# Two transformer blocks on one core: earlier weight loads, both roots ahead of the mixers' tiles, two blocks tile by tile, gate rows in one block

## The reference

```python
def first_block(x, c, ...):                    # 512 tokens, D = 1024
    sh1, sc1, g1, sh2, sc2, g2 = split(silu(c) @ w_ada + b_ada, 6)
    h = rmsnorm(x, norm_attn_g) * (1 + sc1) + sh1
    proj = h @ w_in                            # 3*512 + 4*512 columns, and 8 + 8 for beta and alpha
    y = concat([dilated_attention(...), gated_deltanet(..., beta, alpha)]) @ w_out
    x = x + g1 * y
    h = rmsnorm(x, norm_ffn_g) * (1 + sc2) + sh2
    x = x + g2 * ((silu(h @ w_gate) * (h @ w_up)) @ w_down)
    return rmsnorm(x, final_norm_g)

def second_block(x, c, ctx, c_ctx, ...):       # 512 tokens (main) and 256 (ctx)
    for i in range(2):
        m, mc = the 9 modulations of c and of c_ctx: silu(.) @ w_ada[i] + b_ada[i]
        h, hc = h + 0.5*m[2]*swiglu(norm(h)*(1+m[1])+m[0]), the same for hc     # ffn1, hidden 2816
        z  = (norm(h)*(1+m[4])+m[3]) @ w_in[i]
        zc = the same for hc; in the last layer only the columns of keys and values
        y = concat([fourier, latent attention, spatial gating, pooling])(z, zc) @ w_out[i]
        h = h + m[5]*y;  h = h + 0.5*m[8]*swiglu(norm(h)*(1+m[7])+m[6])         # ffn2
        # hc likewise, except in the last layer
    return rms_norm(h, g_final)
```

## Time and profile before

| | |
|---|---|
| time, median of 3 runs | 3936.7 us (3933.88 to 3936.72) |
| the profiled execution's own time | 3945.08 us |
| its span | 3943.0 us |
| TensorE busy | 3641.0 us, 92% |
| VectorE busy | 2209.7 us, 56% |
| ScalarE busy | 1039.1 us, 26% |
| mean granted TensorE clock | 0.950 of full |
| DMA | 335.83 MB, mean 85 GB/s |

### The profile page before, as it was taken

The page is one execution under the profiler, slowest core; times in us unless marked ns, Lnnn a source line. Parts: engine busy times, 40 slices in busy tenths (PEclk is TensorE's granted clock), DMA queues, the critical chain, the costliest instruction groups (busy, mean ns, idle before and its releaser), DMA issues. The chain is left out here.

```text
span 3943.0 us, 47361 instructions
## 1 busy us (share of the span) xinstructions
PE 3641.0 (92%) x19168; PEld 2981.5 (76%) x19168; DVE 2209.7 (56%) x5139; ACT 1039.1 (26%) x1620; POOL 184.4 (5%) x155
## 2 busy tenths in 40 slices
PE   5898998899989999969999999998999996889998
PEld 3755886788778888856477888887888885568886
DVE  5555555755655656655436666676666535544334
ACT  2354002322332121223333112123212124333222
POOL 1012101000010000010010000010000010000000
PEclk9999887999989999979899999998999998999999
DMA  5533002444323424322012333433343312113332
GB/s 164 153 90 85 1 1 65 118 120 121 107 70 94 113 83 118 90 83 66 11 38 70 92 110 93 113 91 90 87 113 91 107 43 67 57 48 90 95 90 67
DMA packets 636620, 335.83 MB, mean 85 GB/s; under 512 B 20564, under 2 KB 631864, under 8 KB 636145
## 3 DMA queue, kind: packets, MB, share of 16 engines
q1 hardware_dynamic: 635248, 330.19, 29.6%
q10 hardware_dynamic: 1152, 2.62, 0.2%
HBM read 328.05 MB, written 4.72 MB: 84 GB/s over the span
## 5 line engine op out<-in xcount | busy, mean ns | idle before, releaser
L1874 PE MATMUL psum<-hn_high,high 128*128 128x512 f32 (+3 forms) x3336 | 1207.1, 362 | 16.9 <-DVE hn_low L2286 10.4
L1876 PE MATMUL psum<-hn_high,low 128*128 128x512 f32 (+3 forms) x3336 | 1188.2, 356 | 0.0
L1875 PE MATMUL psum<-hn_low,high 128*128 128x512 f32 (+3 forms) x3336 | 1186.2, 356 | 0.0
L1874 PEld LDWEIGHTS psum<-hn_high,high 128*128 128x128 f32 (+2 forms) x3336 | 632.7, 190 | 128.3 <-DVE hn_low L2286 19.2
L1876 PEld LDWEIGHTS psum<-hn_high,low 128*128 128x128 f32 (+2 forms) x3336 | 630.8, 189 | 97.4 <-issue 0.9
L1875 PEld LDWEIGHTS psum<-hn_low,high 128*128 128x128 f32 (+2 forms) x3336 | 631.5, 189 | 90.1 <-issue 0.5
L2311 DVE SCALAR_TENSOR_TENSOR partial<-stage,cond,partial 128x128 f32<-128x128 f32 x2304 | 625.4, 348 | 0.0
L2255 DVE TENSOR_TENSOR low<-stage,high 128x1024 fp32r<-128x1024 f32 (+2 forms) x416 | 498.3, 1218 | 198.5 <-ACT high L1580 198.0
L1580 ACT ACTIVATE high<-stage 128x1024 fp32r<-128x1024 f32 (+2 forms) x416 | 415.5, 1022 | 548.2 <-DMA stage<-in_w_ffn 365.6
L1874 PE MATMUL psum<-hidden_high,high 128*128 128x512 f32 (+1 forms) x1408 | 502.6, 357 | 4.0 <-DVE low L2255 4.0
L1876 PE MATMUL psum<-hidden_high,low 128*128 128x512 f32 (+1 forms) x1408 | 496.1, 352 | 0.0
(11 more groups left out here) (293 smaller groups left out, 3111.4 us busy)
## 6 DMA issues: line engine op xcount, KB each, us to landing
stage<-in_w_ffn SPq DMA_DIRECT2D x240, 512.0 KB, 4.4
stage<-in_w_ada SPq DMA_DIRECT2D x192, 512.0 KB, 4.0
stage<-in_w_in SPq DMA_DIRECT2D x48, 512.0 KB, 5.2
stage<-in_w_out SPq DMA_DIRECT2D x24, 512.0 KB, 4.3
stage<-in_w_ffn SPq DMA_DIRECT2D x32, 384.0 KB, 3.8
stage<-in_w_gate SPq DMA_DIRECT2D x22, 512.0 KB, 4.0
stage<-in_w_up SPq DMA_DIRECT2D x22, 512.0 KB, 5.2
stage<-in_w_down SPq DMA_DIRECT2D x16, 512.0 KB, 4.2
```

The source lines that it names most:

```text
L1874: self.e.matmul(out, high[:, i], xh, start=first and n == 0, stop=False)
L1875: self.e.matmul(out, high[:, i], xl, start=False, stop=False)
L1876: done = self.e.matmul(out, low[:, i], xh, start=False, stop=last and n == nk - 1)
```

## The change

1. **Loads apart from splits.** `load()` issues a block's DMA alone; `load_to(target)` issues loads up to a target as long as a stage is free; `weights()` brings one split block ahead as before, and lets the DMA of one more go.
2. **Norm.** `modulated_norm` brings one block ahead of the root and the second behind it. In `mixers` both roots are taken first, one block is brought ahead of them, `load_mixer`, tables and `clear_pool` come after them, and then the tiles of both parts.
3. **Last square.** The eighth square is no longer added by POOL: PE's `sum_squares` sums `mean_main` (seven squares) and then the last square itself into the same PSUM columns.
4. **Tile by tile in turn.** `products_by_tile` makes the products of two blocks in one pass over the feature tiles: three matmuls of one bank, three of the other. It is used for the gates with qk 0, for gate and up of each swiglu's first group, and for the first two blocks of the mixers.
5. **Gates.** One block of 40 columns: beta in rows 0 to 7, alpha in rows 32 to 39 (and beta's columns once more between them as filling). `gate_rows` now follows qk 0's products. With one call less, the modulations' pumps shift by three.

```diff
-    def bring(self, n):
+    def load(self, n):
...
         self.load_block(n, stage, moves)
+        return stage, raw
+
+    def load_to(self, target):
+
+        while self.loaded <= target and not self.stages.peek().taken:
+            self.landing[self.loaded] = self.load(self.loaded)
+            self.loaded += 1
...
-        self.bring_to(target)
+        later = self.split_after(n + 1)
+        self.bring_to(later[0] if split and later else n)
+        if len(later) > 1:
+            self.load_to(later[1])
...
-            t.free = [("squares", name, k)]
-        part.squares = ("squares", name, k)
-        part.unfinished = k == KT - 1
+            if k < KT - 1:
+                t.free = [("squares", name, k)]
+            else:
+                part.unfinished = t
...
-        self.bring_two()
-        rinv, ready, t = self.residual_root(part, name)
+        self.bring_next(1)
+        rinv, ready, t = root or self.residual_root(part, name)
+        self.bring_next(2)
...
-        for n, name in enumerate(("beta", "alpha")):
...
-            self.linear(name, w, KT, 3584 + 8 * n, 8, part, take_gate)
+        gates, qk = ((3584, 16), (3584, 16), (3592, 8)), ((0, P),)
...
+        self.products_by_tile(keys, [two[0].ap[0:40], two[1].ap], [x[0] for x in asked], [x[2] for x in asked], main.hn,
+                              main.hn_ready)
...
+        for name, row in (("beta", 0), ("alpha", 32)):
+            self.gate_row(name, two[0].ap[row:row + 8], keys[0])
...
-                    self.products(("gate_sum", key), bank_a.ap[:, 0:T], n_a, wa, part.hn, 0, [],
-                                  each=part.hn_ready if at == 0 else None)
...
+                    if at == 0:
+                        self.open_sum(bank_b)
+                        self.products_by_tile([("gate_sum", key), ("up_sum", key)], [bank_a.ap[:, 0:T], bank_b.ap[:, 0:T]],
+                                              [n_a, n_b], [wa, wb], part.hn, part.hn_ready)
...
-        self.load_mixer(layer, base)
+        self.bring_next(1)
+        roots = {}
         for part in both:
...
-            if part in full:
-                self.load_tables(m)
-                self.clear_pool(m)
...
-            self.modulated_norm(name, part, mem.gain[:, :, part.col:part.col + 1], rows(part, 3), [("gain", name)])
+            roots[part.name] = self.residual_root(part, name)
+        self.load_mixer(layer, base)
+        for part in full:
+            m = mem.mixer[part.name]
+            self.load_tables(m)
+            self.clear_pool(m)
+        for part in both:
+            name = ("mix", layer, part.name)
+            self.modulated_norm(name, part, mem.gain[:, :, part.col:part.col + 1], rows(part, 3), [("gain", name)],
+                                root=roots[part.name])
...
+    def products_by_tile(self, keys, outs, numbers, views, x, each):
+
+        nk = len(each)
+        for i in range(nk):
+            for key, out, n, (high, low) in zip(keys, outs, numbers, views):
+                self.wait_ge("split", n)
+                self.wait_ge(*each[i])
+                xh, xl = x[0][:, i, 0:out.shape[1]], x[1][:, i, 0:out.shape[1]]
+                self.e.matmul(out, high[:, i], xh, start=i == 0, stop=False)
+                self.e.matmul(out, high[:, i], xl, start=False, stop=False)
+                done = self.e.matmul(out, low[:, i], xh, start=False, stop=i == nk - 1)
...
-    def sum_squares(self, name, part, bank):
-
-        self.wait_ge(*part.squares)
+    def sum_squares(self, name, part, bank, last):
+
+        self.wait_ge("squares", name, KT - 2)
         self.wait_free(bank)
         for a in range(part.T // P):
-            done = self.e.matmul(bank.ap[:, a:a + 1], part.mean[:, a * P:(a + 1) * P], self.mem.ones[:, 0:1], start=True, stop=True)
+            self.e.matmul(bank.ap[:, a:a + 1], part.mean[:, a * P:(a + 1) * P], self.mem.ones[:, 0:1], start=a == 0, stop=False,
+                          skip_group_check=True)
+        self.wait_ge("square", name, KT - 1)
+        for a in range(part.T // P):
+            done = self.e.matmul(bank.ap[:, a:a + 1], last[:, a * P:(a + 1) * P], self.mem.ones[:, 0:1], start=False, stop=True,
+                                 skip_group_check=True)
```

More of the change, by code:

```diff
@@ L513, in bring_to, with bring_next @@
             self.brought += 1
[L515 to L519, removed]
+    def bring_next(self, count):
+        if self.board.plan is not None:
+            later = self.split_after(len(self.asked))
+            if later:
+                self.bring_to(later[min(count, len(later)) - 1])
+            if len(later) > 1:
+                self.load_to(later[1])
     def pieces(self, name, sources):
@@ L1080, in sections, with opened @@
         w = self.mem.inp["w_in_2"][layer]
-        def product(block, part, n, view, first):
+        def opened(block, part):
             kind, f, columns, _, put = block
             cols = sum(width for _, width in columns)
-            bank, key = self.banks.next(), (kind, layer, part.name, f)
+            bank, key = self.banks.next(), ("sum", (kind, layer, part.name, f))
             self.open_sum(bank)
             out = bank.ap[0:cols, 0:part.T]
-            self.products(("sum", key), out, n, view, part.hn, 0, [] if first else part.hn_ready,
-                          each=part.hn_ready if first else None)
-            return lambda: put(part, f, out, ("sum", key), bank)
-        done = []
-        asked = [self.weights(w, 0, KT, columns, sum(width for _, width in columns)) for _, _, columns, _, _ in blocks[:2]]
-        parts = blocks[0][3]
-        for part in parts:
-            for n, block in enumerate(blocks[:2]):
-                number, slot, view = asked[n]
-                done.append(product(block, part, number, view, n == 0))
-                if part is parts[-1]:
-                    slot.free = [("sum", (block[0], layer, part.name, block[1]))]
-            for take in done:
+            return key, out, lambda: put(part, f, out, key, bank)
+        two = blocks[:2]
+        asked = [self.weights(w, 0, KT, columns, sum(width for _, width in columns)) for _, _, columns, _, _ in two]
+        for part in two[0][3]:
+            keys, outs, takes = zip(*[opened(block, part) for block in two])
+            self.products_by_tile(keys, outs, [x[0] for x in asked], [x[2] for x in asked], part.hn, part.hn_ready)
+            for key, (_, slot, _) in zip(keys, asked):
+                if part is two[0][3][-1]:
+                    slot.free = [key]
+            for take in takes:
                 take()
-            done = []
         for block in blocks[2:]:
@@ L1106, in sections @@
             for part in parts:
-                take = product(block, part, n, view, False)
+                key, out, take = opened(block, part)
+                self.products(key, out, n, view, part.hn, 0, part.hn_ready)
                 if part is parts[-1]:
```

59 lines of the change are left out of this document (37 added, 22 removed).

## The result

| | before | changed |
|---|---|---|
| median | 3935.62 us | 3873.19 us (3868.75 to 3877.88, 4 runs) |
| profiled execution (span) | 3945.08 (3943.0) | 3872.81 (3870.9) |

The ratio is 0.9844, 95% interval 0.9832 to 0.9855: 62.4 us faster by the medians, against 76.7 forecast.

The account below looks back on a forecast made before the run. TensorE, busy 3641.0 of 3943.0 us, bounds the kernel, so only its idle time and clock count. Terms 13.35 + 1.7 + 29.8 + 21.3 + 6.0 + 2.1 + 2.4, say 76.7, take median 3936.7 to 3860.0 us; range 3846 to 3888.

Parts of the forecast that it names:

- The mixers keep less: Rival: third block's late load or second split holds tiles, both layers give back up to 8 us; 3876, chance 0.16.
- The mixers: Both layers' mixers: roots no longer wait for block or main's tiles, products start earlier; 29.8 and 21.3 us.
- The new wait in layer 1: Layer 1's mixers: the third block's split stands behind ctx's tiles, a new wait of 4.1 us.
- does nothing: Rival: something other than the block holds the mixers' root, the first 19.6 us stay; 3895, chance 0.05.
- Loads one block further ahead: Long runs of weight loads: SP's order unchanged, nothing gained or lost; counts only at norms.
- The last square: Norms: one POOL add less before each root, half the column sums run early; 2.1 us a norm, 13.35 without mixers.
- w_out: At w_out: modulation wait of 4.41 us shrinks by 2.1, and the norm's last square gives 2.1.
- The gates: Gates and qk 0: products of both come first, transposes after, so the next block starts earlier; 6.0 us.
- By tile: Two blocks in turn, six matmuls a tile: 1.5 us at first swiglu, 0.9 at ffn2 of layer 1; sum 2.4.
- The rival of a low clock in the turns: Turns between PSUM banks keep 1.2 GHz: 48 matmuls take 19.7 us, not 13.0, at eight pairs; 3914, chance 0.06.
- The split behind the root: Spreads at ffn1 and ffn2 of layer 1 wait less, nothing at w_out; 1.7 us, bounds 0 to 2.

Follow-up runs that it names:

- run 3: Kernel of run 1, but in the mixers constants are issued first, then both blocks, with both splits ahead of the roots: 3898.8 us, 0.9906.
- run 4: Changed kernel, but in the mixers ctx's root is taken behind main's tiles: 3884.4 us, 0.9871.
- run 10: Kernel before plus only the mixers' order: first block, both roots, second block, then constants and all tiles: 3886.0 us, 0.9875.
- run 1: Changed kernel without the further load: weights() brings one split block ahead and issues no load beyond it: 3862.6 us, 0.9817.
- run 5: Changed kernel with the last square added by POOL again and one set of column sums: 3878.6 us, 0.9861.
- run 2: Changed kernel with the gates as before: two blocks of 8 columns, transposes ahead of qk 0, modulations' pumps as before: 3882.3 us, 0.9869.
- run 6: Changed kernel with the loops of products_by_tile swapped, all tiles of one bank and then all of the other: 3871.0 us, 0.9836.
- run 7: Changed kernel with both blocks brought ahead of the roots again in every norm: 3875.1 us, 0.9848.
- run 8: Changed kernel with both roots ahead of ctx's tiles at the two half steps that norm ctx and main: 3857.4 us, 0.9799.

## Why the prediction was right, and where it was not

**The time** lies in the range of 3846 to 3888, but not in the forecast's own of 3851 to 3870. It falls among the times of the rival "The mixers keep less", and for another reason than that rival's: the mixers kept what was forecast, and the loss came where the sum had 0.

**The mixers** carried the forecast, and the mechanism held: 29.2 us at layer 0's first product for 29.8 forecast, 20.0 for 21.3 in layer 1. Runs 3 and 4 show its two halves, 18.1 us a layer for the load ahead of the constants and the split behind the roots, 5.6 a layer for ctx's root, and run 10 shows 48.8 for both alone. The rivals "keep less" and "does nothing" are out. The new wait in layer 1 is 3.15 us for the 4.1 forecast.

**Loads one block further ahead: "Nothing in the long runs"** is the step that failed. I compared SP's rows one with the next and found them alike. But a shift by one pair leaves such rows alike while it puts every bias transfer one pair later, and the pair waits for a stage. The stretch lost 8.5 us against the kernel before. By run 1 the load cost 10.6 us, in the trace 5.6 us of waits and most of the rest low clock behind them. By the prediction's sum this term was 0.

**The last square: "I take 2.1 us a norm"** was mis-sized. The eight records of column sums are one set of four sums for main. The change does not cut that set into two halves; it adds a second set of eight, for the last square alone. At the end of the first block both stand in series behind POOL:

```profile
1107.28 1.87 PE L1943 MATMUL psum<-ones,root 128*128 128x1 f32 x8 [10.55 <-POOL root L1573]
1109.01 1.85 PE L1947 MATMUL psum<-ones,tmp 128*128 128x1 f32 x8
```

By run 5 the last square gave 0.6 us there for 3.6 forecast, at the start 1.2 for 2.0, at the final norm the forecast 1.3, and over the whole kernel 6.9 in the traces and 5.4 in the medians, for about 18 in the sum (13.35, and 2.2 in each mixer).

**w_out** fits its forecast of 4.2 by luck. The modulation's wait was said to shrink by 2.1 us and is gone, 4.4; the last square gave 0.6 for 2.1; and 1.5 us had been lost ahead of it.

**The gates** gave more than the 6.0 forecast, 7.9 on the trace and 8.0 in the trace of run 2. By the medians run 2 is 9.1 us slower, but it also undoes the shift of the modulations. Run 6 shows that the turns with qk 0 are no part of that gain. What is left is the one block and the transposes behind qk 0, which no run tells apart.

**By tile** is near in size, by run 6 1.5 and 1.9 us at the two swiglus for 1.5 and 0.9. The rival of a low clock in the turns is out: the mixers' pair in layer 0 and in layer 1 took 13.64 and 12.65 us, not 19.7. Windows after, granted clock third from the end:

```profile
1708.39:1722.03 13.64, 13.64 (x48) 10.97 (x49) 13.64 (x27) 7.64 (x15) 0.00 (x0) 0.79 0.68 203
3233.51:3246.16 12.65, 12.65 (x48) 9.98 (x48) 12.65 (x25) 6.93 (x13) 0.00 (x0) 0.88 0.65 191
```

The clock rose within both pairs and stayed up to their ends, and run 6 without the turns took the same time. So the clock that goes down and up again in a kernel that cycles through PSUM banks, of which the Trainium skill, "TensorE: Matmul & The Clock Gate", tells under "A second HAM failure mode: psum-queue depth-cycling", did not happen here. It is longer waits that lowered it: the two low windows in the attention (run 1) stand around waits of 3.12 and 2.91 us that the kernel before has not.

**The split behind the root** was near in size: 1.7 in the sum, and 1.9 us by the medians of run 7, which are too close to tell from none. The one place where the traces lead by more is ctx's norm inside the first swiglu, 2.4 us for 0 in the sum, and that did not last to the end of the block, neither in the changed kernel's lead nor in run 7's lag.

The misses by place: too much in the sum were 8.5 us for the attention, 1.5 for the stretch up to w_out's last product, 2.6 for ffn2 of layer 0, 1.9 for the mixers, 1.0 for the end of the first block and 0.7 for the start; too little were 1.9 for the gates, 1.5 for w_out's end and some 0.6 elsewhere. That takes 12.2 from 76.7 and leaves 64.5, which is the traces' lead of 71.4 without the 7 us of the execution of before. The medians are 62.4 apart.

## What to carry to other kernels

A load that is issued earlier is a load that something else in the same queue is issued later: when loads are moved ahead, follow each small transfer that shares the queue to its user, by what stands around it in the user's work and not by its neighbours in the queue. Where one engine's queue holds a small step of part B behind the long work of part A, and another engine waits for it in order, hoisting the small step gives back from half of that wait (5.6 us a mixer, run 4, for a wait of 10.8) to all of it (7.9 us a half step, run 8, for waits of 7.8 and 6.7); look for the same pattern at every stage. Count an added pass on the engine that ends the chain in full, even if it is there to relieve another.

## What the runs showed of the hardware

TensorE's matmuls of 512 columns have two spacings at a granted clock of 1.00. In every profiled execution here they come at 0.233 us up to about 700 us, at the first w_out, and at 0.229 from there on. Only the profiled execution of the kernel before went back to 0.233, from 3549 us to its last product at 3917. Timeline of PE there, and after:

```profile
3898.65 0.40 PE L1874 MATMUL psum<-hidden_high,high 128*128 128x512 f32 x1
...
3899.35 0.40 PE L1874 MATMUL psum<-hidden_high,high 128*128 128x512 f32 x1
```

```profile
3828.93 0.39 PE L1913 MATMUL psum<-hidden_high,high 128*128 128x512 f32 x1
...
3829.62 0.39 PE L1913 MATMUL psum<-hidden_high,high 128*128 128x512 f32 x1
```

Three matmuls in 0.70 and 0.69 us in these rows; over 576 of them 134.17 (from 3681.65) and 131.61 us (from 3616.07), 1.9%. Over these 370 us that is 7 us, which the granted clock does not show, and most of what the profiled execution of before lay above its median. What sets the two spacings stays open.
